# Retention heads 1 to 7: values and gates multiplied as pairs, with seven products for eight in three of eight k-tile pairs

## The reference, cut to what matters

```python
def retention_branch(x, w_in, w_out):
    proj = jnp.einsum('bsd,de->bse', x, w_in)
    q, k, v, gate = jnp.split(proj, [2048, 4096, 8192], axis=-1)
    # 8 heads: q and k 256 wide, rotated; v and gate 512 wide; chunks of 128 tokens
    ...
    o = (inner @ v) + (q @ R) * query_decay
    ...
    o = group_norm_heads(o)
    y = o * jax.nn.silu(gate)
    return jnp.einsum('bse,ed->bsd', y, w_out)

h = layer_norm(DEEPNORM_ALPHA * h + y, ln_gain[i], ln_bias[i])
```

## Time and profile before

| what | value |
|---|---|
| median of three runs | 2363.5 us |
| profiled execution | 2361.91 us |
| its span | 2360.1 us |
| TensorE (PE) | 2344.1 us busy, 11846 matmuls |
| VectorE (DVE) | 1618.9 us |
| ScalarE (ACT) | 1215.5 us |
| GpSimd (POOL) | 424.1 us |
| mean granted TensorE clock | 0.999 |

### The profile page before, as it was taken

One profiled execution on the slowest core, in us unless ns is written; L12 is line 12 of the kernel. 1 busy time (PEld: TensorE's weight loads), 2 busy tenths in 40 slices (PEclk: granted clock), 3 DMA queues, 4 the chain that ended last, 5 costly groups with the idle time before them and its releaser, 6 DMA issues.

```text
span 2360.1 us, 30013 instructions
## 1 busy us (share of the span) xinstructions
PE 2344.1 (99%) x11846; PEld 1975.4 (84%) x11846; DVE 1618.9 (69%) x2008; ACT 1215.5 (52%) x1631; POOL 424.1 (18%) x368
## 2 busy tenths in 40 slices
PE   9999999999999999999999999999999999999999
PEld 7878898888888888888788888887888888888887
DVE  7997578779877777875765656658666655666656
ACT  6876454445544444475655555535444443444542
POOL 1271016326423223400000000001000000000000
PEclk9999999999999999999999999999999999999999
DMA  8655655655665556565566565565655666556653
GB/s 298 196 193 192 214 174 194 191 187 182 212 201 189 188 188 211 199 202 175 179 191 210 163 210 164 178 187 166 197 181 181 217 188 198 180 181 188 185 179 125
DMA packets 127614, 450.38 MB, mean 191 GB/s; under 512 B 14289, under 2 KB 18017, under 8 KB 126961
## 3 DMA queue, kind: packets, MB, share of 16 engines
q1 hardware_dynamic: 127472, 448.46, 59.2%
HBM read 446.26 MB, written 2.15 MB: 190 GB/s over the span
## 4 chain that ended last, share of the span: by engine, by line
PE 95%; DVE 3%; ACT 1%; issue 0%; DMA 0%; POOL 0%; SPq 0%; DVEq 0%; ACTq 0%
PE bank L875 94%; DVE wlo L1747 1%; PE bank L1024 0%; DVE ev L1750 0%; DVE hn L1750 0%; PE bank L1205 0%; PE bank L1276 0%; DVE X L1760 0%; DVE hT L1747 0%; PE bank L1224 0%; DMA hT<-in_xT 0%; DVE S L1747 0%; ACT whi L1290 0%; DVE xa L1747 0%; DVE xa L1750 0%
## 5 line engine op out<-in xcount | busy, mean ns | idle before, releaser
L1747 DVE TENSOR_TENSOR wlo<-raw,whi 128x1024 fp32r<-128x1024 f32 (+2 forms) x811 | 1043.5, 1294 | 644.2 <-ACT whi L1290 642.6
L1290 ACT ACTIVATE whi<-raw 128x1024 fp32r<-128x1024 f32 (+2 forms) x813 | 846.5, 1047 | 878.5 <-PE bank L875 843.2
L875 PE MATMUL bank<-xa,whi 128*128 128x512 f32 (+1 forms) x2688 | 841.6, 395 | 8.5 <-DVE xa L1750 3.4
L875 PE MATMUL bank<-whi,xa 128*128 128x512 f32 x2048 | 639.1, 393 | 2.2 <-DVE wlo L1747 1.8
L875 PEld LDWEIGHTS bank<-xa,wlo 128*128 128x128 f32 x2656 | 497.7, 188 | 115.1
L875 PE MATMUL bank<-xa,wlo 128*128 128x256 f32 (+1 forms) x2656 | 521.1, 278 | 0.0
L875 PEld LDWEIGHTS bank<-whi,xa 128*128 128x128 f32 x2048 | 379.8, 188 | 80.0 <-DVE wlo L1747 2.4
L875 PE MATMUL bank<-whi,xb 128*128 128x512 f32 x1416 | 437.1, 390 | 0.0
L875 PEld LDWEIGHTS bank<-xa,whi 128*128 128x128 f32 x2688 | 410.5, 188 | 16.8 <-issue 10.2
L875 PE MATMUL bank<-wlo,xa 128*128 128x512 f32 x1024 | 399.4, 390 | 0.0
L875 PEld LDWEIGHTS bank<-whi,xb 128*128 128x128 f32 x1416 | 264.8, 188 | 55.3 <-DVE wlo L1747 0.3
(11 more groups left out here) (277 smaller groups left out, 1576.5 us busy)
## 6 DMA issues: line engine op xcount, KB each, us to landing
raw<-in_w SPq DMA_DIRECT2D x803, 512.0 KB, 3.8
hn<-row_sums SPq DMA_DIRECT2D x16, 256.0 KB, 3.8
hT<-in_ln_rows SPq DMA_DIRECT2D x2, 2048.0 KB, 8.1
raw<-in_w SPq DMA_DIRECT2D x9, 256.0 KB, 3.2
S<-in_x SPq DMA_DIRECT2D x4, 512.0 KB, 8.4
hT<-in_x SPq DMA_DIRECT2D x1, 2048.0 KB, 8.0
S<-row_sums SPq DMA_DIRECT2D x16, 128.0 KB, 4.5
out<-S SPq DMA_DIRECT2D x8, 256.0 KB, 2.5
```

The costliest lines, as they stand in the source:

```text
L875: return pe.matmul(o, w, x, start=start, stop=stop, skip_group_check=True)
L1290: act.activation(hi, r, ACT.Copy).then_inc(*w_high(i))
L1747: return dve.tensor_tensor(o, x, y, op)
```

## The change

In heads 1 to 7 the three k-tile pairs 0, 1 and 2 of values and gates are multiplied as groups with seven products, values being the first 512 columns and gates the second. The other five pairs stay plain. Head 0 stays as it was. GpSimd makes the tokens' sums (`mixed`) of these three pairs during head 0, and TensorE reads them in every later head.

A head from 1 on now has 30 pieces in the order: 5 of values, 2 of gates, three groups of `upper`, `lower`, `pair_sums`, `full_sums`, 3 of gates, then queries (4) and keys (4). The gates so end before the queries begin, and the next head's pieces follow on the keys. The steps behind the keys lie beside the next head's values, `ret_gate` seven and `ret_turn` eight positions behind the last key piece. In the last layer norm the rows stand in `hn` and not in `sn`, whose memory the tokens' sums now use, and `load_rows` of that norm lies behind head 7.

```diff
+HEAD_PAIRS = (0, 1, 2)
+PAIRED_HEADS = (1, 2, 3, 4, 5, 6, 7)
+GATE_LEAD, GATE_TAIL = 2, 3
...
+    def paired_head(h):
+        v, g = (begin(kind, h, xa4, "natural", 512) for kind in ("rv", "rgate"))
+        rest = [p for p in range(8) if p not in HEAD_PAIRS]
+        spread = rest[GATE_LEAD:len(rest) - GATE_TAIL]
...
+        for p in rest:
+            use(v, "ret_vg", 1024 * h, 2 * p, 2, p == rest[0], False)
+        for p in rest[:GATE_LEAD]:
+            use(g, "ret_vg", 1024 * h + 512, 2 * p, 2, p == rest[0], False)
+        for i, p in enumerate(HEAD_PAIRS):
+            first, last = i == 0, i == len(HEAD_PAIRS) - 1
+            a = part("upper", 2 * p, first)
+            late(a - 7, "sums", a)
+            part("lower", 2 * p + 1, first)
+            part("pair_sums", 2 * p, first)
+            d = part("full_sums", 2 * p, first, last)
...
+        late(d + 1, "fold", "rv", h, d)
+        late(d + 2, "rv_split", h)
+        for p in rest[len(rest) - GATE_TAIL:]:
+            u = use(g, "ret_vg", 1024 * h + 512, 2 * p, 2, False, p == rest[-1])
...
-            e = block("rgate", h, xa4, "ret_w_in", 4 * D + 512 * h, nat, "natural", 512)
-            late(e + 1, "ret_gate", h)
-            late(e + 2, "ret_turn", h)
+            if h in PAIRED_HEADS:
+                late(e + 7, "ret_gate", h)
+                late(e + 8, "ret_turn", h)
...
+        sums.update({("rv", h): (hflat[:, 0:1024], hflat[:, 1024:2048]) for h in PAIRED_HEADS})
+        rv_sum = [hflat[:, 2048:2560], hflat[:, 2560:3072]]
...
+                    elif step == "fold" and k[0] == "rv":
...
+                        tt(rg[:, 0, :], bank[7][:, :], rv_sum[0], ALU.subtract).then_inc(*vec_val("less", "rv", h))
...
+                        tt(rv_sum[1], rg[:, 0, :], bank[4][:, :], ALU.add).then_inc(*vec_val("fold", "rv", h, 0))
...
+                        tt(rv_sum[0], rv_sum[0], bank[n % 4][:, :], ALU.add).then_inc(*vec_evac("tile", n))
...
+                        tt(rg[:, 1, :], rv_sum[1], bank[6][:, :], ALU.add).then_inc(*vec_val("fold", "rv", h, 1))
...
+                        tt(rv_sum[1], bank[(n + 1) % 4][:, :], rv_sum[1], ALU.subtract).then_inc(*vec_evac("tile", n + 1))
+                        tt(rg[:, 0, :], rg[:, 0, :], bank[6][:, :], ALU.add).then_inc(*vec_val("folded", "rv", h))
...
-                            stt(sn[:, t, 512 * c:512 * c + 512], hn[:, t, 512 * c:512 * c + 512], ALPHA, bank[n % 4][:, :],
+                            stt(hn[:, t, 512 * c:512 * c + 512], hn[:, t, 512 * c:512 * c + 512], ALPHA, bank[n % 4][:, :],
```

More of the change, by code:

```diff
@@ L203, in paired_out, with part @@
         return len(uses) - 1
+    def paired_head(h):
+        v, g = (begin(kind, h, xa4, "natural", 512) for kind in ("rv", "rgate"))
+        rest = [p for p in range(8) if p not in HEAD_PAIRS]
+        spread = rest[GATE_LEAD:len(rest) - GATE_TAIL]
+        def part(name, row, first, last=False):
+            uses.append(Use("ret_vg", 1024 * h, row, 1, 1024, v, first, last, name))
+            return len(uses) - 1
+        for p in rest:
[9 more added lines that the diff above has]
+            d = part("full_sums", 2 * p, first, last)
+            if i < len(spread):
+                use(g, "ret_vg", 1024 * h + 512, 2 * spread[i], 2, False, False)
+        late(d + 1, "fold", "rv", h, d)
+        late(d + 2, "rv_split", h)
+        for p in rest[len(rest) - GATE_TAIL:]:
+            u = use(g, "ret_vg", 1024 * h + 512, 2 * p, 2, False, p == rest[-1])
+        return u
     def mix(u, half, p, sums=0, high=2, low=3):
@@ L416, in layout @@
                 place(n + 7, 5, ("late_gain",))
+            elif h in PAIRED_HEADS:
+                paired_head(h)
             else:
@@ L495, in pieces_in_order @@
         mats[f"pool{g}"] = x["pool_w"][0, g]
+    values, gates = (mats["ret_w_in"][:, c * D:c * D + 2 * D].reshape(D, 8, 512) for c in (2, 4))
+    mats["ret_vg"] = np.concatenate([values, gates], axis=2).reshape(D, 8 * 1024)
     flat, xT = [], x["x"][0].T
@@ L1498, in scalar_program @@
                         q.wait_ge(*pool_val.of("mixed", half, p, 4))
-                        if half and p not in EARLY[1]:
+                        if half == 2:
+                            q.wait_ge(*piece_tile.of("used", ends["fox_out"]))
+                        elif half and p not in EARLY[1]:
                             q.wait_ge(*piece_tile.of("used", XA_FREE[1]))
@@ L1504, in scalar_program @@
                             q.wait_ge(*x_low.of("p", 1))
-                        act.activation(mixed_set(half, p)[:, 0, :], mixed_v, ACT.Copy).then_inc(*x_high("mixed", 11 * half + p))
+                        act.activation(mixed_set(half, p)[:, 0, :], mixing(half)[1], ACT.Copy).then_inc(*x_high("mixed", 11 * half + p))
                     elif step == "fold":
                         kind, c, d = k
+                        if kind == "rv":
+                            if c - 1 in PAIRED_HEADS:
+                                q.wait_ge(*x_low.of("rv", c - 1, 1))
+                            q.wait_ge(*piece_tile.of("used", d))
+                            act.activation(rv_sum[0], bank[5][:, :], ACT.Copy).then_inc(*act_evac("first", "rv", c))
+                            continue
                         if kind == "down0":
@@ L1825, in by_gain @@
             def by_gain(c):
-                x = sn[:, 1, 512 * c:512 * c + 512]
+                x = hn[:, 1, 512 * c:512 * c + 512]
                 q.wait_ge(rows_in, 32)
@@ L2565, in pool_program @@
                             q.wait_ge(*w_low.of(earlier[-1]))
-                        if uses[a].first:
+                        if uses[a].first and uses[a].block.kind != "rv":
                             q.wait_ge(*(x_low.of("ff", 21 if uses[a].block.arg else 0) if uses[a].block.kind == "down0"
```

95 lines of the change are left out of this document (74 added, 21 removed).

## The result

The changed kernel takes 2425.3 us (median of four runs, 2425.0 to 2426.6), the kernel before 2363.5 us: 1.026 times as long, 95% interval [1.0249, 1.0274]. I had forecast 2392 us with 2364 to 2412 as the range. The direction was right, the size was not: + 61.8 us where + 28.7 stood.

What follows compares the result with a forecast made beforehand. The prediction took TensorE's matmuls to bound the kernel from 1700 us on. Waits at four places less the matmuls gone gave + 28.7 us on 2363.5, so 2392 us, range 2364 to 2412.

Steps and rivals of the forecast that it cites:

- What goes: 63 matmuls in heads 1 to 7, 0.2275 us each: 14.3 us off the chain, 2.05 us a head.
- GpSimd and VectorE take turns: GpSimd's additions and VectorE's splits alternate, each waiting for the other whole; additions take 1.6 to 2.0 us on the mean.
- Scores: Before the scores, additions delay VectorE's last two rotation products; TensorE waits 2.1 us (0 to 3) in five heads.
- the walk: Step-by-step estimate of TensorE's waits at four places of a head whose predecessor is paired too (2, 3, 5, 6, 7).
- Transposition: Before the transpositions, earlier arrival and additions beside the gate's products make TensorE wait 3.0 us (1.2 to 3.7).
- Third group: Before the third group's computed pieces, additions behind the freed buffer come late: 2.0 us of wait (0 to 2.9).
- First query piece: Before the first query piece, TensorE waits 0.5 us (0 to 2) for VectorE's fold to empty the values' banks.
- the loads: After group 3's last addition, landing and split take 6.4 us where TensorE has 11.9 before that piece: no wait.
- The sum: Waits less matmuls gone: + 5.55 us in each of five heads, + 0.45 in heads 1 and 4, together + 28.7.
- a granted clock under 0.99: Sign that the forecast is wrong, in the stretch of the heads; no row of before prepares for it.
- 75.8 a head: Sign: the period in heads 2, 3, 5, 6, 7 goes from 70.2 to about 75.8 us.
- the one with late loads: Rival: additions hold the raw buffers, first query pieces wait about 3 us a head more; 2413 us, chance 0.04.

Runs made afterwards that it cites:

- the two best versions: e_best3, 2355.9 us, and the changed kernel with two groups a head, gate's products one piece earlier and first additions waiting for the keys' rotation, 2356.0 us.
- e_best3: Changed kernel with three sums buffers, fold and gate's products one piece earlier, first group's additions waiting for the keys' rotation: 2355.9 us.
- e_bestn: As e_best3, but the first group's additions don't wait for the keys' rotation: 2363.7 us.
- e_noadd: Changed kernel with GpSimd's four additions of a group 32 columns wide instead of 512, all waits kept: 2358.7 us.
- e_fold: Changed kernel with the fold and the values' split one piece earlier: 2405.2 us.
- e_fill: Changed kernel with 14 matmuls that nobody reads before the transpositions' wait in five heads: 2418.2 us.
- e_none: Changed kernel with no head paired, leaving the last norm's new place and the mixing in head 0: 2365.5 us.
- e_3buf: Changed kernel with the sums in three buffers instead of two: 2379.9 us.

## Why the prediction was wrong

*What goes: right.* 0.2275 us for each matmul gone is what the two best versions give back, as their sums above show to about 1 us.

*GpSimd and VectorE take turns: right.* The additions took, with the changed kernel first, then e_best3:

```profile
L2562 POOL TENSOR_TENSOR hT<-raw 128x512 f32<-128x512 f32 x42 | 64.3, 1551 | 202.2 <-DVE wlo L1821 112.3
...
L2562 POOL TENSOR_TENSOR hT<-hT,raw 128x512 f32<-128x512 f32 x42 | 73.3, 1745 | 1.6
```

```profile
L2571 POOL TENSOR_TENSOR hT<-raw 128x512 f32<-128x512 f32 x42 | 72.0, 1733 | 102.2 <-DMA raw<-in_w 89.8
L2571 POOL TENSOR_TENSOR hT<-hT,raw 128x512 f32<-128x512 f32 x42 | 70.0, 1667 | 33.9 <-DVE wlo L1830 32.3
```

1.55 and 1.75 us, within the 1.6 to 2.0 forecast but for 0.05, and no different from the earlier trace rows. The first pair of lines says more in its last column: 112 us of GpSimd's idle time are ended by VectorE's low halves. In e_best3 it is 39, with 7 that its first line doesn't show.

*Scores, 2.1 us: right.* 1.70 drawn, 1.9 with the 0.16. The pair e_bestn and e_best3 shows the cause as the walk had it, in VectorE's products with an addition ahead of each: 2.92 us for the 0.75 of the earlier trace rows.

*Transposition, 3.0 us: right.* 3.13, or 3.3, and both halves of the reason: 1.15 without the additions (e_noadd), the rest from the second group's additions, which start late behind the one buffer. The gate's products beside them:

```profile
1784.83 2.35 DVE L1821 TENSOR_TENSOR S<-S 128x512 f32<-128x512 f32 x2
```

2.35 us for the 1.29 of the earlier trace rows.

*Third group, 2.0 us: near.* 1.14 on the mean in the five heads, 1.3 with the 0.16. In heads 1 and 4 it was 0.74 and 1.83 before two groups: these have no waits ahead of them that give the chain time, and I had put them at the five heads' figure.

*First query piece, 0.5 us, and the loads, "Nothing": wrong.* 2.15 us drawn, two waits, so 2.5. I compared the numbers of operations of TensorE and VectorE and took ScalarE's copy for the fold as there in time. It stands behind splits that wait for a late load. I had computed the load's time for the piece itself, where it does not decide (TensorE has 11.9 us), and not for what is queued behind that split. e_fold gives 20 us back, some 8 of them clock. Over the seven heads this step is 14 us too low; the other three together came out 1.4 lower than forecast. So the waits are 12 of the 33 us that were missing (55 for 43).

*The sum: the failed step.* It took a wait at its idle time. The clock that falls behind the waits, and at which the matmuls after them run, has no term, and is 17 of the 33 us by the stretches at 0.50; e_fill shows 7.1 of it for one of the four places. I had named a granted clock under 0.99 as what would prove me wrong, and said that no row of before prepares for it. That was the mistake: TensorE never waits in the heads of the kernel before, so its trace could not show what a wait costs beyond itself, and an unknown price belongs in the range. With the clock's 17 us the range would have held 2425. The period from scores to scores is 79 to 82 us where the forecast had 75.8 a head.

What is left is 4 us: 1.8 for the part outside the heads, costed at nothing (e_none), whose interval reaches to zero, and 2 without a place.

*Of the rivals* the one with late loads came nearest in time (2413) and named a true part, the raw buffers held by the additions, but at another place. None named what the runs show as the largest lever: the one set of sums. The walk used that reuse twice, in the transposition and in the third group, and never asked what it costs as a whole. One more buffer was worth 45 us, more than the two terms in which it stood, for it also ends the late loads and the stretches at the lower clock (28 us of waits, 17 of clock).

Open stays why the clock held at waits of 1.70 and 1.76 us in e_3buf and fell behind 1.38 and 0.76 in the changed kernel, and why it did so in head 2 and not in head 3, behind 1.41 and 0.76. By these runs the length of a wait alone doesn't tell what it costs.

## What to carry to other kernels

A stage that has never waited can't tell what a wait costs: when a change brings TensorE waits of a few microseconds in a dense stretch, price the matmuls behind them at the lower clock too, or at least let the range hold it. If a computed operand is made by a chain (load, addition, split, matmul), look first for the buffer whose reuse closes the chain, and give it a third one before moving anything else; then clear the queue positions one by one, each by its own row: what stands behind a split that waits for a load, and which short VectorE products lie beside GpSimd's long ones. The number of groups was no steady lever: in the given order two a head, with a plain piece between them, cost 4 us and three 62, and once their waits were cleared both gained 7.

## What the runs showed of the hardware

- The granted clock falls to 0.50 for microseconds of full work not only behind a wait of 3.13 us but also behind two of 1.38 and 0.76 us with 0.5 us of work between; behind 1.41 and 0.76 us in the next head it stays at 1.00.
- 14 matmuls that nobody reads, in place of a wait of equal length, make the kernel 7.1 us faster in five places.
- A VectorE product with two SBUF inputs of 0.37 us takes 1.46 when a 1.27 us addition of GpSimd goes first (2.92 for 0.75, two of each). Holding GpSimd back for 1 us takes 1.70 us of TensorE's wait away in each of five heads and adds 0.27 at another place.
- Two additions in a row on VectorE take 1.28 us, on GpSimd 2.54 alone and, over the changed kernel's heads, 3.1 to 3.5 on the mean beside VectorE's work.
